# Six small matmuls of a recurrence, moved from one block behind the sixth score bank to pairs behind the third, fourth and fifth

## The reference, cut to what matters

```python
kk = heads(k * k_k)
kk = kk * lax.rsqrt(jnp.maximum(jnp.sum(kk * kk, axis=-1, keepdims=True), 1e-24))
...
def step(S, inp):
    sa = jnp.einsum('bhvk,bhk->bhv', S, -kk_t)
    S = S * w_t[:, :, None, :] + sa[..., None] * (kk_t * a_t)[:, :, None, :] + v_t[..., None] * k_t[:, :, None, :]
```

## Time and profile before

| What | us |
|---|---|
| Median of 3 runs | 3595.08 |
| Span of the profiled execution, first to last instruction | 3593.4 |
| PE busy in the span | 3366.4 |
| DVE, ACT, POOL busy | 1629.7, 1029.4, 1100.8 |
| Unit 3 (odd, with the sums), c0 to the next unit's c0 | 44.79 |
| Unit 2 (even, without) | 44.75 |

### The profile page before, as it was taken

One profiled execution on the slowest core, in us unless ns is written; L12 is line 12 of the kernel. 1 busy time (PEld: TensorE's weight loads), 2 busy tenths in 40 slices (PEclk: granted clock), 3 DMA queues, 4 the chain that ended last, 5 costly groups with the idle time before them and its releaser, 6 DMA issues.

```text
span 3593.4 us, 75635 instructions
## 1 busy us (share of the span) xinstructions
PE 3366.4 (94%) x32810; PEld 2517.2 (70%) x32810; DVE 1629.7 (45%) x2736; ACT 1029.4 (29%) x1689; POOL 1100.8 (31%) x720
## 2 busy tenths in 40 slices
PE   8987899879979999989999989999999999989998
PEld 3435678633337766778888875558888888868886
DVE  3246742321127877544334361125666666633333
ACT  3033232211124245341111131243333333242221
POOL 0052142123322100143223220025555555334441
PEclk9998899889989999999999999999999999989999
DMA  4311054259962300121111114430000000012221
GB/s 159 129 47 77 24 200 176 83 203 380 360 263 88 131 13 2 71 94 59 70 49 71 71 48 175 150 140 11 15 15 15 15 15 11 3 71 94 106 101 52
DMA packets 63384, 346.39 MB, mean 96 GB/s; under 512 B 17323, under 2 KB 17339, under 8 KB 26321
## 3 DMA queue, kind: packets, MB, share of 16 engines
q1 hardware_dynamic: 40608, 293.62, 21.1%
q0 software_dynamic: 18736, 36.94, 3.0%
q10 hardware_dynamic: 3712, 11.01, 0.8%
HBM read 379.77 MB, written 28.84 MB: 114 GB/s over the span
## 4 chain that ended last, share of the span: by engine, by line
PE 81%; DVE 7%; ACT 4%; DMA 3%; issue 3%; POOL 1%; ACTq 0%; DVEq 0%; POOLq 0%
PE psum L469 24%; PE psum L481 11%; PE psum L482 11%; PE psum L483 11%; PE psum L2370 4%; PE psum L3321 3%; ACT arena L885 2%; PE psum L2397 2%; PE psum L3304 1%; PE psum L499 1%; PE psum L3608 1%; DMA ring<-in_wall,arena 1%; DVE stat L942 1%; PE psum L495 1%; PE psum L2703 1%
## 5 line engine op out<-in xcount | busy, mean ns | idle before, releaser
L469 PE MATMUL psum<-arena 64*64 64x64 f32 (+5 forms) x13464 | 642.5, 237 | 53.5 <-issue 14.4
L469 PEld LDWEIGHTS psum<-arena 64*64 64x64 f32 (+2 forms) x13464 | 532.4, 141 | 123.1 <-issue 88.7
L529 POOL TENSOR_TENSOR ring_low<-ring,slab_high 128x2048 fp32r<-128x2048 f32 x66 | 303.9, 4619 | 599.4 <-ACT slab_high L522 599.4
L481 PE MATMUL psum<-h_high,slab_high 128*128 128x512 f32 (+1 forms) x1008 | 357.4, 355 | 2.6 <-POOL ring_low L529 2.6
L482 PE MATMUL psum<-h_low,slab_high 128*128 128x512 f32 (+1 forms) x1008 | 357.2, 354 | 0.0
L483 PE MATMUL psum<-h_high,ring_low 128*128 128x512 f32 (+1 forms) x1008 | 357.0, 354 | 0.0
L469 PE MATMUL psum<-arena,ring 128*128 128x512 f32 (+3 forms) x880 | 335.6, 541 | 1.8 <-DVEq L1431 1.0
L469 PEld LDWEIGHTS psum<-arena,ring 128*128 128x128 f32 (+2 forms) x880 | 163.2, 187 | 170.6 <-issue 161.6
L1092 DVE TENSOR_TENSOR arena<-arena,psum 128x512 f32<-128x512 f32 x66 | 39.5, 598 | 470.3 <-PE psum L483 466.1
L481 PEld LDWEIGHTS psum<-h_high,slab_high 128*128 128x128 f32 x1008 | 191.0, 190 | 29.5 <-POOL ring_low L529 2.8
L482 PEld LDWEIGHTS psum<-h_low,slab_high 128*128 128x128 f32 x1008 | 191.1, 190 | 26.2
(11 more groups left out here) (519 smaller groups left out, 6263.7 us busy)
## 6 DMA issues: line engine op xcount, KB each, us to landing
ring<-in_wall SPq DMA_DIRECT2D x181, 1024.0 KB, 5.7
arena<-in_wall SPq DMA_DIRECT2D x96, 1024.0 KB
spill<-arena ACTq DMA_DIRECT2D x8, 768.0 KB, 11.2
arena<-spill POOLq DMA_DIRECT2D x16, 384.0 KB, 3.5
filters<-arena POOLq DMA_DIRECT2D x2, 2048.0 KB, 6.7
arena<-filters POOLq DMA_DIRECT2D x2, 2048.0 KB, 14.5
arena<-moe_out POOLq DMA_DIRECT2D x8, 512.0 KB, 7.0
arena<-in_tabs POOLq DMA_DIRECT2D x2, 1536.0 KB, 11.5
```

The source lines that it names most:

```text
L469: last = L.eng.matmul(out, a, b, start=(i == 0), stop=(i == len(pairs) - 1))
L481: L.eng.matmul(out, a_hi, b_hi, start=(i == 0), stop=False)
L529: L.eng.tensor_tensor(m.low[:, n % SLOTS, :], m.ring[:, n % SLOTS, :], m.high_of(n).bitcast(F32), ALU.subtract).then_inc(m.sem("slab_split ...
```

## The change: three pairs in place of one block

```diff
+SUMMED_AT = (2, 3, 4)
+def removal_bank_tensor(L, m):
+    ps = L.next_bank()
+    for bank_free, count in L.bank_frees:
+        L.eng.wait_ge(bank_free, count)
+    return ps, L.bank_full
+def removal_tile_tensor(L, m, u, ps, full, t):
+    if t == 0:
+        L.eng.wait_ge(m.sem("kk_squares"), L.nth("kk_squares"))
+    last = L.eng.matmul(ps[:, 2 * t:2 * t + 2], u.ka[:, t * P:(t + 1) * P], m.tab("heads64")[:, 0:P:CH], start=True, stop=True)
+    if t == TT - 1:
+        last.then_inc(full, 1)
...
+            if sums and at_bank == SUMMED_AT[0]:
+                removal = removal_bank_tensor(L, m)
             scores.append(squares_tensor(L, hh, lambda *at: [(feat(lhs, *at), feat(rhs, *at))], n))
+            if sums and at_bank in SUMMED_AT:
+                for t in range(2):
+                    removal_tile_tensor(L, m, after, *removal, 2 * (at_bank - SUMMED_AT[0]) + t)
             if before is not None:
                 chain_tensor(L, m, B, before, at_bank)
             at_bank += 1
-        if after is not None and after.d == 0 and at_bank == 6:
-            removal_sum_tensor(L, m, B, after)
...
-    for _ in range(6 * (1 if before is None else 2)):
+    for _ in range(SUMMED_AT[0] * (1 if before is None else 2)):
         L.next_bank()
```

More of the change, by code:

```diff
@@ L3656, in unit_tensor @@
     scores = []
+    sums = after is not None and after.d == 0
     for lhs, rhs, n in ((u.be, u.al, TT), (u.ka, u.al, TT), (u.be, u.rh, TX), (u.ka, u.rh, TX)):
         for hh in range(2):
+            if sums and at_bank == SUMMED_AT[0]:
+                removal = removal_bank_tensor(L, m)
             scores.append(squares_tensor(L, hh, lambda *at: [(feat(lhs, *at), feat(rhs, *at))], n))
+            if sums and at_bank in SUMMED_AT:
+                for t in range(2):
+                    removal_tile_tensor(L, m, after, *removal, 2 * (at_bank - SUMMED_AT[0]) + t)
             if before is not None:
@@ L3736, in unit_scalar @@
         removal_root_scalar(L, m, B, after)
-    for _ in range((FIRST - 6) * (1 if before is None else 2)):
+    for _ in range((FIRST - SUMMED_AT[0]) * (1 if before is None else 2)):
         L.next_bank()
@@ L3816, in unit_vector @@
         L.eng.sem_inc(m.sem("starts_read"), 1)
+    if after is not None and after.d == 0:
+        L.next_bank()
+        removal_rooted = L.read_out
     for hh in range(2):
@@ L3823, in unit_vector @@
             chain(4 + 2 * k + hh)
-        if after is not None and after.d == 0 and k == 0:
-            L.next_bank()
-            removal_rooted = L.read_out
     if u.d == 0:
```

## The result

The changed kernel takes 3600.49 us, the median of 19 runs (3596.10 to 3606.94). The kernel before, run beside it, takes 3594.24 us (19 runs, 3582.40 to 3601.20). The ratio is 1.0023, with a 95% interval of 1.0016 to 1.0031: 8.3 us slower (5.8 to 11.1), where I forecast 2.0. The loss stands just beyond the bound of 0.2% between no change and slower, and its interval holds that bound. The two medians by themselves lie 6.25 us apart, a ratio of 1.0017.

A forecast was written before the change was run, and what follows sets the result against it. PE's list was taken to bound the kernel, 81% of the span. Per unit 1.09 + 0.92 - 1.57 = 0.44 us, 3.1 in seven, less 1.1 relief: +2.0, giving 3597.1 us, range 3586 to 3605.

The forecast's parts named there:

- The path: Whole kernel: the chain of waits runs through PE for 81% of the span, so PE's list sets the time.
- The pairs: c1 to c4 in the seven odd units: three pairs of sum matmuls at 0.63 us each add 1.09 us a unit.
- The bank stall: At c5, waiting for ACT to free the sums' bank: c4 to c5 takes 1.68 us, adding 0.92 a unit.
- extra drain: At ACT's table load, by the skill's page: a drain making the stall an estimated 1.1 us longer a unit.
- The block: c5 to c7: 3.09 us with the sums' block, 1.52 without it, so 1.57 us removed a unit.
- 0.8 us steps: Sign behind c5: c6 and c7 should follow in steps of 0.8 us at the high clock.
- The direct loss: Seven odd units at an unchanged clock: 0.44 us more a unit, 3.1 us in all.
- the price of the clock: TensorE's clock falls in the seven odd units: costs 17 to 28 us, taken as 22, and stays.
- one relief: Stall within the low-clock stretch: the low clock costs nothing there, 3.2 us at most, a third counted, 1.1.
- third rival: Between c3 and c5 the clock falls earlier and stays low longer: 3604.8 us if in all seven units; chance 0.17.
- The rule on gaps: The skill's page on gaps between matmul bursts: pairs alone leave the clock alone, the new stall would endanger it.

The follow-up runs named there:

- E3: The kernel before without the six sum matmuls and their bank, ACT's root taken of numbers already in `stat`: 3569.53 us, 0.9934 of before.
- E5: The kernel before, its block behind c5, each of the six matmuls streaming 64 columns instead of 2: 3582.04 us, 0.9968 of before.
- E6: The changed kernel with 64 columns instead of 2 for each of the six matmuls, the stall kept: 3596.65 us, 1.0022 of before.
- E10: The kernel before, unchanged, run again for another profile: 3587.8 us.
- E1: The changed kernel with ACT's table loaded early by a small root of a constant ahead of the sums: 3595.74 us, 1.0009 of before.
- E7: The changed kernel with 64 columns for each of the six matmuls and ACT's table loaded early: 3581.13 us, 0.9965 of before.
- E8: The changed kernel, unchanged, run again for a second profile: 3600.75 us, 1.0022 of before.
- E11: The kernel before, unchanged, run once more for its seven units with sums: 3592.0 us.
- E12: The changed kernel, unchanged, run once more for its seven units with sums: 3605.96 us.
- E4: The changed kernel with three matmuls each behind s2 and s3, not two each behind s2, s3 and s4: 3597.21 us, 1.0009 of before.

## Why the prediction was right in kind and short in size

- **The path.** Right: PE's list sets the time, and the change acts in the seven odd units alone: the even units from 2 to 14 add up to 311.9 to 312.5 us before and 312.2 to 313.0 after, but for the first profile's 316.9, with its pause in unit 14. E3 and E5 show how much hangs on the seven.
- **The pairs.** c1 to c4 took 4.25 us at the high clock where 4.08 was worked out and 2.99 stood before: +1.26 a unit instead of +1.09.
- **The bank stall.** c5 waits for ACT in seven of seven units. The step is 1.78 instead of the 1.68 of the sum, so +1.02 instead of +0.92. The table load did take 1.28, with the root 0.01 behind it. The extra drain of the Trainium skill (ScalarE: Activation LUTs, section What ACT_TABLE_LOAD costs) again doesn't show: its estimated 1.1 us more a unit would have made the idle time of 0.98 about 2.1.
- **The block.** c5 to c7 takes 0.71 + 0.78 = 1.49 at the high clock (unit 7 of E6), where it took 3.09: 1.60 removed, against 1.57. In the changed kernel itself the 0.8 us steps that I had named as a sign didn't come: the clock had fallen by then, and c6 and c7 mostly took 0.88 and 1.14. The direct loss is 1.26 + 1.02 - 1.60 = 0.68 a unit and 4.8 in all, instead of 3.1; the 0.66 of E6 agrees.
- **The clock: the step that was mis-sized.** The prediction said "the price of the clock is thus 17 to 28 us; I take 22. It stays, with one relief". Measured against E5, the price before is 317.15 - 299.1 = 18.1 in that first profile, 9.5 in E10 and 13.8 in E11: 13.8 in the mean, some 0.3 us for each us at the low clock and not the 0.5 that was read from units 3 and 5. After the change the three executions average 319.1, and 299.1 + 4.8 of that is no clock: its price is 15.2. The term is +1.4 against the mean of before, where -1.1 stood. Against the first profile alone it is -2.9, and the whole change is 319.1 - 317.15 = +1.9, just the +2.0 of the sum. The sum was right for the execution that it was made on; that execution was no mean of the kernel.
- **The price was read too high.** The reading of units 3 and 5 put unit 3 at 7.2 us of low clock from a rounded mean; the trace has 6.83. It also took the dearest step for all of them: a unit of before takes an estimated 42.6 without a fall (E5), 43.7 with 3.41 us at the low clock, 44.8 with 6.83 and 46.3 with 10.24.
- **The relief was too small, and the longer fall was left out.** The relief was there, and larger than the third that I counted: E1 has no stall and as much low clock (58.0 us, the mean of the three), and its seven units are 3.4 us shorter, where the stall's 1.02 a unit makes 7.1. So an estimated 3.7 us of the stall cost nothing, going by one execution of E1. But the low clock lasts 15 us longer in all, some 4.7 us at 0.32 each, and that stood in the third rival and not in the sum.
- **The third rival was half right.** Over three executions each, the fall came 5.17 us behind c0 after the change and 6.61 before, and the clock stayed low for 8.3 us a unit against 6.2; 9 of 21 units have the long stretch, where it was 3 of 21. But a unit with the long stretch is on average 1.1 us longer than one without (46.2 against 45.1), not 1.54; that fits with the stall lying in the low time.
- **The rule on gaps.** The Trainium skill (TensorE: Matmul & The Clock Gate, section Why this matters for your kernels) warns of idle gaps of PE between bursts of matmuls. The prediction read the new stall into that, but the gaps that the page names are longer than these 0.98 us; by it neither the pairs nor the stall would touch the clock. Both do here: E1 has seven falls without any stall, and E6 four with the stall, where E7 has none without it.

In sum: 6.2 us of the measured 8.3 (5.8 to 11.1) are found in the seven units, 4.8 of them direct and 1.4 by the clock. Where the other 2 us lie, if they are real, wasn't settled: the medians are only 6.25 apart, three profiles each are too few, and the 1.4 hangs on the three of before, which are 8.5 us apart. Also, the stretches ahead of unit 1 and behind unit 15 vary by one to several us between executions of one kernel. Why a unit of before is low for 3.41 us in one execution and for 10.24 in another stays open too.

## What to carry to other kernels

Read the clock of several executions before pricing a change near a fall: one profile of this kernel could be 4 us dearer than the mean in seven short places. When a bank is taken earlier, ask the order who takes it next, and what its reader has to do first; a table load that was free while the bank's next user came eight turns later cost some 5 us once that user stood one score bank and one chain step behind. Where matmuls of few columns can't be avoided, try to widen what they stream: here a block with 64 columns took 1.55 us instead of 1.50, and the clock stayed up.

## What the runs showed of the hardware that was not expected

Twelve records that stream 64 columns behind 128x128 weights took 1.55 us against 1.50 with 2 columns, and the clock stayed at 1.00 in all seven units instead of falling in all seven. That is worth 11.5 us. The mean granted clock of all eight timed runs agrees (0.963 to 0.966, against 0.958 to 0.962 in the 24 of before).

PE also pauses at times without any semaphore behind it. This is the one in unit 14 of the changed kernel's first profile:

```profile
3052.39 0.68 PE L469 MATMUL psum<-arena 64*64 64x64 f32 x16 [0.74 <-issue]
```

The clock fell 1.8 us later and stayed low for 10.2 us; the unit took 46.93 instead of 43.26. E7 had the same pause of 0.74 and the same fall there, and E8, E10, E11 and E12 had neither. But E4 had the pause too, and its clock stayed at 1.00:

```profile
3051.28 0.68 PE L469 MATMUL psum<-arena 64*64 64x64 f32 x16 [0.74 <-issue]
```

Its unit 14 took 43.62. So the pause by itself costs some 0.4 us, and the fall follows it in two of three cases. What brings the pause about was not tried.
